# Up-projection weights loaded with a cast instead of converted beforehand, and late adaLN blocks moved behind an earlier sample tile

## The chip, the cores and the metric

The kernel runs on eight cores of one Trainium2 chip, the same program on each. A core has one prompt sequence (2048 tokens) and 16 sample sequences of 8 tokens (128 tokens). No data passes between the cores. The time is the device time in microseconds of the slowest core, as a median over runs; less is better. TensorE multiplies matrices, VectorE, ScalarE and GpSimd work on tiles, SyncE (SP) only issues transfers.

## The reference, cut to what matters

One layer with width 1024. Modulation vectors come from a conditioning vector (adaLN, six parts of 1024). Then a mixer with two halves, a gated linear recurrence and a short convolution, and an MLP with squared ReLU:

```python
mod = silu(c) @ w_ada + b_ada                       # sh1, sc1, g1, sh2, sc2, g2
h = rms_norm(x) * (1 + sc1) + sh1
q, fz, i, g, gb, gc, hv = split(h @ w_in)           # 7 blocks of 512 columns
logf = log(lb + (1 - lb) * sigmoid(fz)); k = 1 - exp(logf)
o, s_new = recurrence(q, k, logf, i, s0)            # 4 heads, state 128 x 128, chunks of 64 (8 for samples)
o_rec = rms_per_head(o) * g_onorm * silu(g)
o_conv = gb * short_conv(gc * hv)                   # width 3
x = x + g1 * (concat[o_rec, o_conv] @ w_out)
h2 = rms_norm(x) * (1 + sc2) + sh2
x = x + g2 * (square(relu(h2 @ w_up)) @ w_down)
y = rms_norm(x) * g_final
```

Prompt states start at zero; each sample sequence has its own start state (16 x 256 KB a core, read and written back).

## The kernel before, in words

**Stages.** First four blocks of `w_ada` are loaded and turned into shift and scale of the mixer. Then nine mixer tiles follow: eight prompt tiles of 256 tokens (p0 to p7) and one sample tile (s) of 128 tokens, in the order of the list `tiles` (line 1091). p0 and p1 run interleaved, the others follow each other, with `norm1` of the next tile put in front of each. A tile's projections come in the order F (forget gate, weight block 1), V (2), Q (0), G (3), then the recurrence R, then C (5), H (6), B (4), then the output projection. Its result goes to a DRAM scratch (`x1`). Last come six groups of up to three blocks of 128 tokens: `norm2`, `up` (8 weight blocks, in the order 1, 2, 0, 3, 5, 6, 4, 7), `down` (8 blocks).

**Weights in SBUF.** Every block of 128 x 4096 lies in DRAM as fp32 (2 MB) and in SBUF as bf16 (1 MB). A transfer that casts is issued by GpSimd. `wup` 0 to 6 takes the place of `win` 0 to 6, `wup7` that of `wout0`, so an up block can be loaded when the last prompt tile has read the projection block beneath it. `wdn` 0 and 1 lie where two `w_ada` buffers (`adaR`, line 563) and the ring of sample states (`SlR`, line 566) also lie; `wdn` 3 to 7 lie where tile buffers of the mixer were.

**Loads of the kernel before.** `convert(i)` (line 631) casts block i of `w_up` from DRAM to a bf16 scratch in DRAM (`wscr`), issued by GpSimd; `load_up` (line 636) copies it into SBUF on SP's queue, 1 MB. All eight up blocks go this way. `load_dn` (line 639) casts straight into SBUF, on GpSimd. The list `CONV` (line 1093) says how many conversions are written behind each tile; the first of a tile waits for the 21st TensorE operation of that tile, the others are given an empty slice of the list (it has fewer than 100 entries) and wait for no TensorE operation. Blocks 6 to 11 of `w_ada` (shift, scale and gate of the MLP) are loaded two at a time while p2 and p3 run: `late_mod` and `gates(1)`.

**What sets the order.** Every operation is written down with its reads, writes and a cost; `schedule` (line 125) then runs an event model and fixes the order of each engine's queue, first ready and then first written first. Each engine works through its queue in that order and waits in front of an operation whose inputs are not there. The model has transfers share the DMA engines: a transfer takes its bytes at 330 GB/s, GpSimd's queue gets 80% while SP or ScalarE has one too (lines 45 to 47, 147 to 151). An operation that reads what a transfer brings is planned 4 us after it. GpSimd's transfer number k waits for number k-6 (`SWDGE_DEPTH`, line 107). Dependences go by buffer names, so all of `modT` is one buffer: who reads any of it waits for every earlier write.

The profile names lines of helpers: L404 and L415 are matmuls and transposes, L431 ScalarE, L438, L442, L444, L448 and L452 VectorE or GpSimd, L465 transfers.

Of the kernel before, what the change touches and what calls it, by code (L numbers as in the profile page):

```python
# [368 lines left out]
def build_program():  # L369
    nc = bass.Bass("TRN2", target_bir_lowering=False)  # L370

    def din(name, shape):
        return nc.dram_tensor(name, shape, F32, kind="ExternalInput").ap()
# [8 lines left out]
    wup_d = din("w_up", [8, 128, 4096]); wdn_d = din("w_down", [8, 128, 4096])  # L382
# [3 lines left out]
    wscr_d = nc.dram_tensor("wscr", [16, 128, 4096], BF16, kind="Internal").ap()  # L386
# [3 lines left out]
    P = Prog(nc)  # L390
# [7 lines left out]
    def mm(specs, r, w, prio=None):  # L398
        specs = list(specs)

        def fn(e):
            ins = None
            for (o_, l_, r_, st, sp_) in specs:
                ins = e.matmul(o_, lhsT=l_, rhs=r_, start=st, stop=sp_, skip_group_check=True)  # L404
            return ins
        c = sum(max(nfree(s[2]) * 0.4167 + 2.5, 25.0) for s in specs)
        return P.op("pe", fn, r, w, c, prio=prio)
# [29 lines left out]
    def tt(eng, out, in0, in1, op, r, w, prio=None, mode=1.0):  # L437
        return P.op(eng, lambda e: e.tensor_tensor(out=out, in0=in0, in1=in1, op=op), r, w, vec_cost(eng, out, mode), prio=prio)  # L438

    def ts(eng, out, in0, s1, s2, op0, op1, r, w, prio=None, mode=2.0):  # L440
        if op1 is None:
            f = lambda e: e.tensor_scalar(out=out, in0=in0, scalar1=s1, scalar2=None, op0=op0)  # L442
        else:
            f = lambda e: e.tensor_scalar(out=out, in0=in0, scalar1=s1, scalar2=s2, op0=op0, op1=op1)  # L444
        return P.op(eng, f, r, w, vec_cost(eng, out, mode), prio=prio)
# [17 lines left out]
    def dma(eng, out, in_, r, w, nbytes, prio=None, after=()):  # L463
        c = {"pool": 1000.0, "sp": 600.0, "act": 100.0}[eng]
        o = P.op(eng, lambda e: e.dma_start(out=out, in_=in_), r, w, c, dma=float(nbytes), prio=prio)  # L465
        o.preds += [(d, True) for d in after]
        return o

    UPORD = (1, 2, 0, 3, 5, 6, 4, 7)
# [51 lines left out]
    wup, wup_n = [], []  # L521
# [46 lines left out]
    wdn, wdn_n = [], []  # L568
# [47 lines left out]
    MB2 = 1024 * 512 * 4  # L616
    ada_slot = {}
    flat = lambda t: t[:].rearrange("p k n -> p (k n)")

    def load_ada(j):  # L620
        t, n = (ada0R if j < 4 else adaR).take()
        ada_slot[j] = (t, n)
        dma("pool", flat(t), wada_d[j], [], [n], MB2)

    def load_in(j):
        dma("pool", flat(win[j]), win_d[j], [], [win_n[j]], MB2)
# [4 lines left out]
    def convert(i, after):  # L631
        dma("pool", wscr_d[i], wup_d[i] if i < 8 else wdn_d[i - 8], [], ["wscr%d" % i], 1.5 * MB2, after=after)

    up_ops = {}

    def load_up(j):
        up_ops[j] = dma("sp", flat(wup[j]), wscr_d[j], ["wscr%d" % j], [wup_n[j]], MB2 / 2)

    def load_dn(j):
        gate = up_ops.get(4 if j == 2 else 7)  # L640
        dma("pool", flat(wdn[j]), wdn_d[j], [], [wdn_n[j]], MB2, after=[gate] if gate else ())


    dma("pool", cB[:, 0:256], cB_d[:, 0:256], [], ["cB"], 128 * 1024)
# [29 lines left out]
    def mod_block(bi, first, j0, out_j0):  # L674
        if first:
            mod_bank[0] = UR.take()
        bank, bn = mod_bank[0]
        t, n = ada_slot[bi]
        c0 = 0 if first else 68
        for cj in range(4):  # L680
            col = c0 + cj * 17
            mm([(bank[:, col:col + 17], t[:, k, cj * 128:(cj + 1) * 128], scT[:, k, :], k == 0, k == 7) for k in range(8)],
               [n, "scT"], [bn])
        if not first:
            tt("dve", modT[:, out_j0:out_j0 + 8, :], bank[:, 0:136].rearrange("p (a b) -> p a b", b=17),
               badaT[:, j0:j0 + 8].unsqueeze(2).to_broadcast([128, 8, 17]), ALU.add, [bn, "vecT"], ["modT"])
            if out_j0 in (8, 24):
                ts("dve", modT[:, out_j0:out_j0 + 8, :], modT[:, out_j0:out_j0 + 8, :], 1.0, None, ALU.add, None, ["modT"], ["modT"])

    def gate_half(bi, g, half, gt, gt_n):  # L690
        t, n = ada_slot[bi]
        bank, bn = UR.take()
        mm([(bank[0:17, :], scT[:, k, :], t[:, k, :], k == 0, k == 7) for k in range(8)], [n, "scT"], [bn])
        c0 = half * 512
        tt("dve", gt[0:17, c0:c0 + 512], bank[0:17, :], gt[0:17, c0:c0 + 512], ALU.add, [bn, gt_n], [gt_n])

    def gates(g):
        gt, gt_n = xrR.take()
        src = bg_d[g * 1024:(g + 1) * 1024]
        dma("sp", gt[0:17, :], src.partition_broadcast(17), [], [gt_n], 17 * 4096)  # L700
        for half in range(2):
            gate_half((4 if g == 0 else 10) + half, g, half, gt, gt_n)
        dma("sp", gate_d[:, g * 1024:(g + 1) * 1024], gt[0:17, :], [gt_n], ["gated%d" % g], 17 * 4096)
# [37 lines left out]
    def norm1(kind, ti):  # L741
        hi = (0, 2, 1)[hcnt[0]] if hcnt[0] < 3 else (hcnt[0] + 1) % 2
        h, hn = hT[hi], "hT%d" % hi
        hcnt[0] += 1
        if kind == "s":
            nbv, nbn = normed(xs_d[:, :], [])
            sample_mod(nbv, nbn, h, hn, 0, 0, 8)
            return h, hn
        nbs = [normed(xp_d[(ti * 2 + b) * 128:(ti * 2 + b + 1) * 128, :], []) for b in range(2)]
        for jh in range(2):  # L750
            M, Mn = NR.take()
            Mb = M[:, :].bitcast(BF16)
            for b in range(2):
                tr([(Mb[:, j * 256 + b * 128:j * 256 + (b + 1) * 128], nbs[b][0][:, (jh * 4 + j) * 128:(jh * 4 + j + 1) * 128], ident)
                    for j in range(4)], [nbs[b][1], "cB"], [Mn])
            for j in range(4):
                jj = jh * 4 + j
                ts("dve", h[:, jj, :], Mb[:, j * 256:(j + 1) * 256], modT[:, 8 + jj, 0:1], modT[:, jj, 0:1], ALU.mult, ALU.add,
                   [Mn, "modT"], [hn], mode=1.0)
        return h, hn  # L760
# [327 lines left out]
    mod_block(3, False, 8, 8)  # L1088
    for j in (1, 2, 0, 3, 5, 6, 4):
        load_in(j)  # L1090
    tiles = [("p", 0), ("p", 1), ("p", 2), ("p", 3), ("s", 0), ("p", 4), ("p", 5), ("p", 6), ("p", 7)]
    hs = {}
    CONV = {5: 2, 6: 2, 7: 3, 8: 1}
    hs[0] = norm1(*tiles[0]); hs[1] = norm1(*tiles[1])
    load_ada(4); load_ada(5)
    load_out(0)
# [3 lines left out]
    conv_i = 0  # L1100

    def gen(n_):
        kind, ti = tiles[n_]
        return mixer_tile(kind, ti, kind == "p" and ti == 7, hs[n_][0], hs[n_][1], SAMPLE if kind == "s" else ti * 2)
# [9 lines left out]
    for g_ in (g0, g1):  # L1114
        for _ in g_:
            pass
    load_ada(6); load_ada(7)

    def late_mod(q):
        for i in range(2):  # L1120
            mod_block(6 + 2 * q + i, i == 0, 24 + 8 * q, 16 + 8 * q)

    for n_ in range(2, len(tiles)):
        t0op = len(P.ops)
        if n_ + 1 < len(tiles):
            hs[n_ + 1] = norm1(*tiles[n_ + 1])
        for step in gen(n_):
            if n_ == 2 and step == "Q":
                late_mod(0)
                load_ada(8); load_ada(9)  # L1130
            if n_ == 2 and step == "B":
                late_mod(1)
                load_ada(10); load_ada(11)
            if n_ == 3 and step == "Q":
                gates(1)
            if step == "B" and n_ + 1 == len(tiles):
                WB = View(wall[2:6])
                for j in UPORD[:7]:
                    load_up(j)
                norm2(bgroups[0])  # L1140
        pe_ops = [o for o in P.ops[t0op:] if o.eng == "pe"]
        for i in range(CONV.get(n_, 0)):
            convert(UPORD[conv_i], pe_ops[20 + 80 * i:21 + 80 * i])
            conv_i += 1
        if n_ == 6:
            load_dn(0); load_dn(1)
    load_up(7)
    load_gates(1)
    dma("sp", gfin_b[:], gfin_d.partition_broadcast(128), [], ["gfin_b"], 128 * 4096)
    for j in range(2, 8):  # L1150
        load_dn(j)
# [65 lines left out]
```

How the kernel before makes its waits and increments, by code:

```python
            def run(e, h):  # L325
                for o in order[e]:
                    for key, (val, d) in need_of[o.idx].items():
                        if d.chan is not None:
                            h.wait_ge(csem[key], val * 16)
                        else:
                            h.wait_ge(esem[key], d.cnt)
                    ins = o.fn(h)
                    if o.chan is not None:
                        ins.then_inc(csem[o.chan], 16)
                    elif o.signal:
                        ins.then_inc(esem[e], 1)
                if e == "sp":
                    for c, n in self.chans.items():
                        h.wait_ge(csem[c], n * 16)
```

## Time and profile before

| | |
|---|---|
| median of 3 runs | 929.48 us (927.96 to 930.94) |
| profiled execution | 927.96 us |
| its span, slowest core (5) | 926.4 us |
| spans of the cores | 914.6 to 926.4 us |
| TensorE busy | 826.0 us (89%) |
| VectorE, ScalarE, GpSimd busy | 466.9, 366.2, 166.8 us |
| DMA | 113.93 MB in packets, HBM read 129.56 MB |

Busy TensorE is a union of pipelined matmuls. The profile cuts the span in 40 slices of 23 us; TensorE is at nine tenths or more in most of them from the fourth on, and falls to 6 tenths with a granted clock of 6 tenths of full speed in the slice that begins near 417 us. The DMA engines are at 7 to 9 tenths in the first ten slices, at 3 and 4 in the next two, at 6 to 9 up to some 510 us, and at 0 to 2 from there.

### The profile page before, as it was taken

How to read it: one execution, taken by the hardware profiler on the slowest of the kernel's cores; microseconds unless marked ns; L12 is line 12 of the kernel's file. 1: busy time of each engine (PE TensorE's matmuls, PEld its weight loads, DVE VectorE, ACT ScalarE, POOL GpSimd, SP SyncE). 2: the span in 40 equal slices, each digit the busy share in tenths (PEclk: the TensorE clock that was granted, in tenths of full speed). 3: DMA queues.
4: the chain of work that ended last, by engine and by line, in shares of the span. 5: the costliest groups of instructions: out<-in, count | busy, mean ns of one | idle time of the engine just before them, and what ended most of it. 6: DMA issues, size and time to landing. Idle time of an engine off the chain costs nothing.

```text
span 926.4 us, 16715 instructions; the slowest of 8 cores (914.6 to 926.4 us)
## 1 busy us (share of the span) xinstructions
PE 826.0 (89%) x5929; PEld 513.6 (55%) x5929; DVE 466.9 (50%) x851; ACT 366.2 (40%) x780; POOL 166.8 (18%) x218
## 2 busy tenths in 40 slices
PE   0147999999898999986999999999999999999995
PEld 0124876777676657653654565456446545644862
DVE  0023597667879687685443445234514533442421
ACT  2036558374747567632330333133214312311411
POOL 2000022332153342242201200200120021002001
PEclk9997999999999999996999999999999999999998
DMA  8999789999346668798996211210221012002001
GB/s 161 215 183 196 137 161 162 201 181 235 112 149 239 140 174 201 188 241 187 227 195 157 95 43 47 91 69 2 91 69 46 24 46 91 2 1 83 31 2 45
DMA packets 27436, 113.93 MB, mean 123 GB/s; under 512 B 3845, under 2 KB 4229, under 8 KB 22362
## 3 DMA queue, kind: packets, MB, share of 16 engines
q0 software_dynamic: 4848, 39.19, 26.8%
q1 hardware_dynamic: 17610, 55.85, 18.9%
q10 hardware_dynamic: 4896, 17.83, 6.2%
q8 instruction: 48, 0.79, 0.3%
q14 instruction: 34, 0.28, 0.1%
HBM read 129.56 MB, written 30.88 MB: 173 GB/s over the span
## 4 chain that ended last, share of the span: by engine, by line
PE 75%; DVE 6%; DMA 6%; issue 6%; ACT 5%; ACTq 0%; POOL 0%; DVEq 0%; POOLq 0%
PE G L404 41%; PE U L404 23%; PE O L404 9%; DMA win_44<-w_in 5%; PE M L415 1%; DMA cB<-constB 1%; ACT W_140 L431 1%; DVE Sd_85 L438 1%; DVE h2T L444 1%; PE M L404 1%; DVE Ts_84 L438 1%; ACT Sb_86 L431 1%; ACT W_142 L431 0%; ACT W_141 L431 0%; ACT W_139 L431 0%
## 5 line engine op out<-in xcount | busy, mean ns | idle before, releaser
L444 DVE TENSOR_SCALAR h2T<-M,modT 128x128 bf16<-128x128 bf16 x128 | 43.9, 343 | 23.7 <-PE M L415 13.7
L431 ACT ACTIVATE W_140<-G 128x384 f32<-128x384 f32 (+2 forms) x38 | 19.7, 519 | 52.3 <-PE G L404 52.3
L415 PE MATMUL M<-cB,W_135 128*128 128x128 bf16 (+1 forms) x144 | 13.3, 231 | 30.1 <-DVE lnoml L438 20.9
L431 ACT ACTIVATE W_135<-xn_145 128x1024 bf16<-128x1024 f32 x17 | 17.9, 1053 | 45.6 <-PE M L415 36.2
L431 ACT ACTIVATE W_136<-xn_146 128x1024 bf16<-128x1024 f32 x17 | 17.9, 1053 | 25.7 <-PE M L415 15.8
L438 POOL TENSOR_TENSOR xr_147<-xr_147,W_138 128x512 f32<-128x512 f32 x8 | 10.5, 1312 | 97.1 <-DVE W_138 L438 96.9
L415 PEld LDWEIGHTS M<-cB,W_135 128*128 128x128 bf16 (+1 forms) x144 | 9.9, 104 | 32.6 <-issue 31.2
L431 ACT ACTIVATE Sb_86<-Sd_85 128x512 bf16<-128x512 f32 x16 | 10.0, 627 | 37.8 <-DVE Sd_85 L438 37.8
L438 POOL TENSOR_TENSOR xr_147<-xr_147,W_137 128x512 f32<-128x512 f32 x5 | 6.3, 1267 | 102.6 <-DVE W_137 L438 102.6
L438 DVE TENSOR_TENSOR uT<-W_138,G 128x384 bf16<-128x384 f32 (+1 forms) x26 | 13.7, 528 | 17.2 <-ACT W_138 L431 16.6
L404 PE MATMUL G<-hT_60,win_44 128*128 128x256 bf16 x128 | 18.4, 303 | 4.4 <-DMA win_44<-w_in 4.4
L431 ACT ACTIVATE W_137<-G 128x384 f32<-128x384 f32 (+1 forms) x24 | 11.4, 475 | 25.8 <-PE G L404 25.0
L438 DVE TENSOR_TENSOR Ts_84<-Sd_85,U 128x512 f32<-128x512 f32 x31 | 21.1, 682 | 0.7
L431 ACT ACTIVATE W_140<-W_140 128x512 f32<-128x512 f32 x32 | 20.1, 630 | 2.1
L404 PE MATMUL G<-wdn_129,uT 128*128 128x512 bf16 x88 | 20.8, 379 | 0.0
L404 PE MATMUL G<-wdn_128,uT 128*128 128x512 bf16 x88 | 20.8, 379 | 0.0
L404 PE MATMUL G<-wdn_127,uT 128*128 128x512 bf16 x88 | 20.8, 379 | 0.0
L404 PE MATMUL G<-wdn_130,uT 128*128 128x512 bf16 x88 | 20.8, 379 | 0.0
L438 DVE TENSOR_TENSOR uT<-W_137,G 128x384 bf16<-128x384 f32 (+1 forms) x24 | 12.9, 537 | 15.6 <-ACT W_137 L431 14.1
L431 ACT ACTIVATE W_138<-G 128x384 f32<-128x384 f32 (+1 forms) x26 | 12.2, 469 | 21.0 <-PE G L404 21.0
L438 DVE TENSOR_TENSOR uT<-W_139,G 128x384 bf16<-128x384 f32 (+1 forms) x24 | 13.0, 542 | 14.5 <-ACT W_139 L431 14.5
L438 DVE TENSOR_TENSOR W_138<-U,Gp 128x512 f32<-128x512 f32 x16 | 11.0, 687 | 16.3 <-PE U L404 15.0
(565 smaller groups left out, 2149.0 us busy)
## 6 DMA issues: line engine op xcount, KB each, us to landing
wscr<-w_up POOLq DMA_DIRECT2D x8, 1024.0 KB, 14.9
xn_146<-x ACTq DMA_DIRECT2D x9, 512.0 KB, 4.7
xn_145<-xp ACTq DMA_DIRECT2D x8, 512.0 KB, 11.0
xn_146<-xp ACTq DMA_DIRECT2D x8, 512.0 KB, 9.6
ada_111<-w_ada POOLq DMA_DIRECT2D x4, 1024.0 KB, 13.4
ada_112<-w_ada POOLq DMA_DIRECT2D x4, 1024.0 KB, 22.5
xn_145<-x ACTq DMA_DIRECT2D x8, 512.0 KB, 3.4
xr_148<-xp SPq DMA_DIRECT2D x6, 512.0 KB, 14.7
```

The costliest lines, as they stand in the source:

```text
L404: ins = e.matmul(o_, lhsT=l_, rhs=r_, start=st, stop=sp_, skip_group_check=True)
L415: ins = e.transpose(out=o_, in_=i_, identity=id_)
L431: return P.op("act", lambda e: e.activation(out=out, in_=in_, func=func, **kw), r, w, c, prio=prio)
L438: return P.op(eng, lambda e: e.tensor_tensor(out=out, in0=in0, in1=in1, op=op), r, w, vec_cost(eng, out, mode), prio=prio)
L444: f = lambda e: e.tensor_scalar(out=out, in0=in0, scalar1=s1, scalar2=s2, op0=op0, op1=op1)
```

## The change

The order of the engines is planned by the same `schedule` with the same costs. What is written down changes:

- up blocks: `load_up` casts straight from fp32 into SBUF on GpSimd's queue (2 MB read); no conversion of `w_up` is left.
- down blocks 4 to 7 are converted in DRAM beforehand (`CONV` is now a list of scratch blocks 12 to 15), one behind each of the tiles number 5 to 8 of the list (counted from 0), each waiting for the 21st TensorE operation of its tile; `load_dn` copies them on SP's queue, each chained to the SP transfer written before it. Down blocks 0 to 3 stay casting loads on GpSimd; 0 and 1 are written behind tile number 7.
- the sample tile comes fourth instead of fifth.
- blocks 6 to 11 of `w_ada` are loaded behind the tiles number 4, 5 and 6; their matmuls come behind tiles 5 and 6, `gates(1)` behind tile 7. As `adaR` shares SBUF with `SlR`, they can be loaded only when the sample tile is through with its states.

```diff
     def load_up(j):
-        up_ops[j] = dma("sp", flat(wup[j]), wscr_d[j], ["wscr%d" % j], [wup_n[j]], MB2 / 2)
+        dma("pool", flat(wup[j]), wup_d[j], [], [wup_n[j]], MB2)

     def load_dn(j):
-        gate = up_ops.get(4 if j == 2 else 7)
-        dma("pool", flat(wdn[j]), wdn_d[j], [], [wdn_n[j]], MB2, after=[gate] if gate else ())
+        if 8 + j in CONV:
+            dma("sp", flat(wdn[j]), wscr_d[8 + j], ["wscr%d" % (8 + j)], [wdn_n[j]], MB2 / 2, after=[o for o in P.ops if o.dma and o.eng == "sp"][-1:])
+        else:
+            dma("pool", flat(wdn[j]), wdn_d[j], [], [wdn_n[j]], MB2)
...
-    tiles = [("p", 0), ("p", 1), ("p", 2), ("p", 3), ("s", 0), ("p", 4), ("p", 5), ("p", 6), ("p", 7)]
+    tiles = [("p", 0), ("p", 1), ("p", 2), ("s", 0), ("p", 3), ("p", 4), ("p", 5), ("p", 6), ("p", 7)]
-    CONV = {5: 2, 6: 2, 7: 3, 8: 1}
+    CONV = [12, 13, 14, 15]
...
-    load_ada(6); load_ada(7)
-
-    def late_mod(q):
-        for i in range(2):
-            mod_block(6 + 2 * q + i, i == 0, 24 + 8 * q, 16 + 8 * q)
-
     for n_ in range(2, len(tiles)):
...
         for step in gen(n_):
-            if n_ == 2 and step == "Q":
-                late_mod(0)
-                load_ada(8); load_ada(9)
-            if n_ == 2 and step == "B":
-                late_mod(1)
-                load_ada(10); load_ada(11)
-            if n_ == 3 and step == "Q":
-                gates(1)
...
-        pe_ops = [o for o in P.ops[t0op:] if o.eng == "pe"]
-        for i in range(CONV.get(n_, 0)):
-            convert(UPORD[conv_i], pe_ops[20 + 80 * i:21 + 80 * i])
+        mark = [o for o in P.ops[t0op:] if o.eng == "pe"][20:21]
+        if n_ in (5, 6):
+            for i in range(2):
+                mod_block(4 + 2 * (n_ - 4) + i, i == 0, 24 + 8 * (n_ - 5), 16 + 8 * (n_ - 5))
+        if n_ == 7:
+            gates(1)
+            load_dn(0); load_dn(1)
+        if n_ in (4, 5, 6):
+            load_ada(6 + 2 * (n_ - 4)); load_ada(7 + 2 * (n_ - 4))
+        if 5 <= n_ and conv_i < 4:
+            convert(CONV[conv_i], mark)
             conv_i += 1
-        if n_ == 6:
-            load_dn(0); load_dn(1)
```

## Rows read from the trace of the kernel before

**Rows 1.** Spans of the cores: span, mean granted TensorE clock.

```profile
core 5: 926.4 us, clock 0.979
```

**Rows 2.** Busy us by stretch: length, PE, PEld, DVE, ACT, POOL, clock, DMA share, GB/s.

```profile
120.00:240.00 120.00, 116.65 (x1189) 86.10 (x1188) 88.91 (x157) 69.78 (x142) 33.98 (x55) 1.00 0.93 188
240.00:320.00 80.00, 70.61 (x660) 52.27 (x657) 64.02 (x115) 52.35 (x107) 34.02 (x44) 0.98 0.50 153
320.00:400.00 80.00, 75.89 (x651) 54.01 (x649) 61.47 (x99) 53.80 (x105) 25.50 (x38) 1.00 0.78 196
400.00:437.00 37.00, 25.48 (x163) 13.79 (x162) 27.01 (x49) 11.02 (x24) 12.82 (x12) 0.77 1.00 192
437.00:520.00 83.00, 82.22 (x463) 44.09 (x462) 31.06 (x65) 20.03 (x44) 9.94 (x11) 1.00 0.77 171
```

**Rows 3.** Waits of TensorE, 400 to 437 us: us in total, times, longest.

```profile
PE U L404 <- POOL mix_152 L438: 2.8, 1, 2.8
```

**Rows 4.** DMA queues: packets, MB, share of 16 engines over the span.

```profile
q0 software_dynamic: 4848, 39.19, 26.8%
q1 hardware_dynamic: 17610, 55.85, 18.9%
```

**Rows 5.** DMA issues, 437 to 520 us: KB each, us from issue to landing.

```profile
wdn_129<-w_down POOLq DMA_DIRECT2D x1, 1024.0 KB, 15.8
...
wdn_134<-w_down POOLq DMA_DIRECT2D x1, 1024.0 KB, 48.5
...
gfin_b<-g_final SPq DMA_DIRECT2D x1, 512.0 KB, 27.1
```

**Rows 6.** GpSimd in order of time: start us, us, what.

```profile
443.23 0.60 POOL L465 DMA_DIRECT2D wdn_129<-w_down  x1 [7.23 <-DMA recp<-rout]
...
450.99 0.57 POOL L465 DMA_DIRECT2D wdn_134<-w_down  x1
```

**Rows 7.** TensorE in order of time, tiles p6 and p7 and first MLP group.

```profile
323.82 1.91 PE L404 MATMUL G<-hT_60,win_44 128*128 128x256 bf16 x16
...
364.34 1.04 PE L404 MATMUL G<-hT_61,win_44 128*128 128x256 bf16 x8
...
375.03 1.91 PE L404 MATMUL G<-hT_61,win_44 128*128 128x256 bf16 x16
...
379.47 1.89 PE L404 MATMUL G<-win_45,hT_61 128*128 128x512 bf16 x8
...
398.22 1.89 PE L404 MATMUL U<-wout_50,mix_83 128*128 128x512 bf16 x8
...
410.21 1.04 PE L404 MATMUL G<-hT_61,win_47 128*128 128x256 bf16 x8
...
437.02 4.06 PE L404 MATMUL G<-h2T,wup_53 128*128 128x384 bf16 x24
...
473.42 1.46 PE L404 MATMUL U<-h2T,wup_59 128*128 128x384 bf16 x8
...
517.16 1.89 PE L404 MATMUL O<-wdn_134,uT 128*128 128x512 bf16 x8
```

**Rows 8.** Waits of GpSimd, whole span: us in total, times, longest.

```profile
POOL win_48 L465 <- DMA adaf_109<-w_ada: 10.6, 1, 10.6
```

**Rows 9.** GpSimd in order of time, two places.

```profile
316.35 0.59 POOL L465 DMA_DIRECT2D wdn_127<-w_down  x1 [5.02 <-DMA recs<-Sl_119]
...
396.81 0.72 POOL L438 TENSOR_TENSOR mix_83<-W_137,sg_80 128x256 bf16<-128x256 f32 x1
```

**Rows 10.** TensorE in order of time: a late adaLN block and half a gate.

```profile
170.18 0.96 PE L404 MATMUL U<-scT,ada_111 128*128 128x17 bf16 x32
...
211.49 1.90 PE L404 MATMUL U<-ada_111,scT 128*17 128x512 bf16 x8
```

**Rows 11.** DMA issues, 110 to 250 us: KB each, median us to landing.

```profile
ada_112<-w_ada POOLq DMA_DIRECT2D x3, 1024.0 KB, 21.0
```

**Rows 12.** Waits of TensorE, whole span.

```profile
PE U L404 <- DMA adaf_109<-w_ada: 10.1, 1, 10.1
```

More of the change, by code:

```diff
@@ L632, in convert @@
         dma("pool", wscr_d[i], wup_d[i] if i < 8 else wdn_d[i - 8], [], ["wscr%d" % i], 1.5 * MB2, after=after)
-    up_ops = {}
     def load_up(j):
-        up_ops[j] = dma("sp", flat(wup[j]), wscr_d[j], ["wscr%d" % j], [wup_n[j]], MB2 / 2)
+        dma("pool", flat(wup[j]), wup_d[j], [], [wup_n[j]], MB2)
     def load_dn(j):
-        gate = up_ops.get(4 if j == 2 else 7)
-        dma("pool", flat(wdn[j]), wdn_d[j], [], [wdn_n[j]], MB2, after=[gate] if gate else ())
+        if 8 + j in CONV:
+            dma("sp", flat(wdn[j]), wscr_d[8 + j], ["wscr%d" % (8 + j)], [wdn_n[j]], MB2 / 2, after=[o for o in P.ops if o.dma and o.eng == "sp"][-1:])
+        else:
+            dma("pool", flat(wdn[j]), wdn_d[j], [], [wdn_n[j]], MB2)
     dma("pool", cB[:, 0:256], cB_d[:, 0:256], [], ["cB"], 128 * 1024)
```

## The prediction

> **What bounds the kernel now.** I read the spans of the cores first: core 5 is the slowest, 926.4 us at a mean granted clock of 0.979 [rows 1]. The profiled execution took 927.96 us, so 1.6 us lie outside the span, and the median of the three runs, 929.48 us, is 1.5 us above it. The sum below is made against 927.96 and then moved up by those 1.5 us.
>
> The busy time by stretch is the second view, and the reader should see three stages in it [rows 2]. From 520 us on (the MLP groups) the matmul engine hardly idles; the same weights lie in SBUF in both kernels, so nothing of this change reaches that part. From 120 to 400 us (mixer tiles) it is nearly full: idle 3.35 of 120 us, then 9.4 of 80 around the sample tile, then 4.1 of 80. From 400 to 437 us, the end of the last prompt tile, 11.5 of 37 us are idle and the granted clock is 0.77, a mix of 2.4 and 1.2 GHz after the engine had begun to wait. So all that can be won before the MLP is about 28 us of idle time and a few us at the lower clock. The waits of that last stretch are the third view: the longest is 2.8 us for GpSimd's product into `mix` [rows 3], the rest are links of the same chain on VectorE and ScalarE, and no weight load stands in the list.
>
> The queues are the fourth view [rows 4]. 26.8% of 926.4 us for 37 casting transfers on GpSimd's queue (39.19 MB written) is 248 / 37.4 = 6.6 us of all sixteen engines for each. The plain queue of SP takes 18.9% for 55.85 MB, 3.1 us a MB, so 3.3 us for a 1.05 MB block that is already bf16.
>
> **The change, part by part.**
>
> *Up weights.* Eight plain copies of 3.3 us on SP become eight casting loads of 6.6 us on GpSimd; 26 us more engine time, in the stretch where the DMA share is 1.00 already [rows 2]. What pays for it: eight conversions in DRAM go, four (of `w_down`) come, and four `w_down` loads become plain copies. Do the loads come late? In the kernel before, six casting loads that follow each other land between 443.23 + 15.8 = 459.0 and 450.99 + 48.5 = 499.5 us, 8.1 us apart [rows 5, 6]. The first weight block is free when its last reader in tile p7 ends, 376.9 us, the second at 381.4, the seventh at 411.3 [rows 7]. At 15.8 us for the first and 8.1 for each further one they land at 393, 401, 409, 417, 425, 433 and 441, and with one conversion between (449) the eighth, free at about 437, lands at 457. They are needed from 437.0, one each (473.42 - 437.02) / 7 = 5.2 us, the eighth at 473.4 [rows 7]. The tightest has 16 us left: cost 0. The work that hides them is the rest of tile p7. The two `w_down` blocks behind them land by 465 and 473, and are needed from about 517.2 - 5 x 5.2 = 491 [rows 7]. The four plain copies are chained behind the copy of the final gain, which took 27.1 us from its issue near 440 [rows 5]: 467, then even 10 us each gives 507 for the last, needed at 517 [rows 7].
>
> *GpSimd's order.* GpSimd issues in order, and its DMA number k waits until number k-6 has landed. Such a wait is seen at the start: 10.6 us in front of `win_48` for a load six issues back [rows 8]. There nothing stood behind it. In tile p7 eleven issues now stand between GpSimd's products into `mix` and its residual adds, for which the output projection waits. Most find their sixth predecessor long landed. One does not: the last conversion comes six behind the second up load. The order is planned with 2 MB at 330 GB/s and 80% of the engines, 7.9 us a load with 3.1 us of overhead in all, so this load lands at about 377 + 2 x 7.9 + 3 = 395 in the plan; by the rows it is 401. The plan can thus put the conversion in front of the product that ends at 397.5 and that the output projection at 398.2 waits for [rows 7, 9]. A wait of some 5 us there stops TensorE for 5 us, as the kernel before shows in small at 316.35, where a `w_down` issue held an add back for 5.0 us [rows 9]. Bounds: 0 if the conversion is planned elsewhere, 10.6 by the wait at the start. I take +5.
>
> *Late adaLN blocks.* Blocks 6 to 11 are loaded behind the sample tile now, since their two buffers share SBUF with the sample states. A prompt tile less ahead of it, 364.34 - 323.82 = 40 us [rows 7], and the landing of the sample tile's last store, at 316 us in the kernel before [rows 9], comes near 276. Then follow load, matmuls, load, matmuls, load, gates: three rounds. TensorE's own work is the same, 4 x 0.82 us and 2 x 1.9 us [rows 10], about 7 us. A round's second load takes 21.0 us to land [rows 11]; the plan allows about the same. `norm1` of p6 and p7 also waits for these blocks, as one buffer name covers all of `modT`; 276 + 21 = 297 and some 320 lie ahead of 323.8 and 364.3, where their projections begin, so this is covered. What is left is TensorE standing in front of a block that is late. Bounds: 0, and 10.1, the longest wait for such a block at the start [rows 12]. I take +2, nearer to the stretch 120 to 240 us, where six of these loads passed without such a wait.
>
> *Relief in the early tiles.* Three ungated conversions and six adaLN loads leave 120 to 240 us, where the DMA share is 0.93 [rows 2]. The engine idles 3.35 us there, mostly behind VectorE and ScalarE. Bounds -3.35 and 0; I take -1.
>
> *Moved work.* The 7 us of adaLN matmuls go from a stretch with 3% idle to one with 8% (13.5 of 160 us) and can lie in its gaps. The sample tile takes its 9.4 us of gaps along. Bounds -9.4 and +9.4, as these gaps can shrink or repeat; I take -2, a third of the moved work hidden.
>
> Sum: 0 + 5 + 2 - 1 - 2 = +4 us, 927.96 + 4 = 932.0 for such an execution, 933.5 us as a median.
>
> **A rule against the change.** The rows around 437 to 520 us give a casting load 8.1 us beside plain copies [rows 5, 6]. The Trainium skill, "DMA: Bandwidth & Descriptors", section "Queues, rings and completion order", says that each DMA engine takes turns between the rings that have work, packet by packet. By that rule GpSimd's queue would get half while SP's or ACT's has work, not the 80% of the plan. The pace that this would give is the first rival; the 8.1 us agree with it only where the plain queues are mostly empty.
>
> **The rivals.**
>
> *Weights late, slower.* If a casting load gets half of the engines during the whole of tile p7, it takes 13.2 us [rows 4]: 393, 406, 419, 432, 446, 459, then the conversion at 472, the seventh at 485, the eighth at 498. The sixth still makes it (needed at 463), the seventh is 17 us late and the eighth 25 us: 958 us, or 953 with part of it made up. It decides from about 10 us a load. For it: the DMA share of 1.00 in 400 to 437 [rows 2]. Against: the plain queues lose the eight copies in this very stretch, and have only residual blocks left.
>
> *Faster.* The plain queue, free of eight copies, and ScalarE's issues behind it no longer lengthen the chain of 400 to 437 us; 5 of its 11.5 idle us go, with 3 us of the early relief: 921.5 us. For it: idle time and the clock in that stretch [rows 2, 3]. Against: the longest wait there ends with GpSimd, whose queue gets more to do.
>
> *No change.* The loads were hidden and are hidden again, and the orders differ without effect: 929.5 us. For it: no wait for an up weight before, a margin of 16 us after. Against: the order of every engine is planned anew, and 28 us of gaps can move.
>
> **How the numbers follow.** The forecast gets 0.44, late weights 0.10, faster 0.28, no change 0.18. Within 0.3% (2.8 us) is what a measurement of this kernel cannot tell from no change; 0.06 of the forecast's chance lies there, so slower is 0.38 + 0.10 = 0.48, same 0.24, faster 0.28. The likeliest case's own range is 929 to 941. Its lower end must go on to the faster case with some of the gaps closed, 917, and its upper end to most of the late weights, 951.
>
> **What would show it.** Right: in the profile after, GpSimd waits several us in front of `wscr`, with `mix` products behind it and TensorE waiting for `mix` in tile p7; no wait of TensorE for `wup`; DMA share well under 0.9 in the early tiles and near 1 from 270 to 470 us; the first up matmul some 4 us later than 437. Wrong: a wait for `wup` or `wdn` (late weights), a first up matmul before 433 (faster), or a start of the MLP that moved for another reason, such as gaps at the sample tile.

## The result and the profile after

The changed kernel takes 958.69 us as a median (955.48 to 962.98, 4 runs), the kernel before 928.72 us beside it: 1.0326 times as long, interval 1.0274 to 1.0377. It is slower, as was likeliest, but by 30 us where 4 were forecast, and outside the range. In some executions the cores of one die run at a lower granted clock and the time is longer; all ratios here, and the medians given for e10 and e14, are over the other executions. The profiled execution, 962.98 us, is the longest of the four; its slowest core is core 2, against [rows 1].

```profile
core 2: 961.4 us, clock 0.960
```

The busy time by stretch has the columns of [rows 2] (length, PE, PEld, DVE, ACT, POOL, clock, DMA share, GB/s), so that each row can be held against its counterpart.

```profile
120.00:240.00 120.00, 107.56 (x1067) 81.42 (x1076) 101.58 (x174) 76.23 (x154) 48.64 (x64) 0.96 0.51 153
240.00:320.00 80.00, 76.23 (x701) 55.74 (x707) 56.80 (x98) 47.54 (x96) 27.17 (x37) 1.00 0.50 124
320.00:400.00 80.00, 73.76 (x673) 54.54 (x677) 52.92 (x91) 47.42 (x100) 27.47 (x37) 0.99 0.88 168
400.00:437.00 37.00, 28.74 (x201) 19.08 (x202) 26.07 (x51) 11.17 (x23) 6.79 (x11) 0.78 1.02 178
437.00:520.00 83.00, 50.24 (x281) 27.96 (x280) 23.32 (x47) 19.09 (x42) 7.12 (x8) 0.79 0.89 199
```

The last row is the place. TensorE idles 32.8 of 83 us there, 0.8 before. From 120 to 437 us little is lost in sum: 120 to 240 us lose 9.1 (the sample tile lies there now), 240 to 320 win 5.6, 320 to 400 lose 2.1, 400 to 437 win 3.3. TensorE in order of time around 437 us (start, us, what, idle time before and its releaser) shows how it stops.

```profile
434.26 4.06 PE L404 MATMUL G<-h2T,wup_53 128*128 128x384 bf16 x24
...
448.12 2.72 PE L404 MATMUL U<-h2T,wup_54 128*128 128x384 bf16 x8 [8.50 <-DVE W_137 L438]
...
454.74 1.46 PE L404 MATMUL U<-h2T,wup_52 128*128 128x384 bf16 x8
...
480.76 2.72 PE L404 MATMUL G<-h2T,wup_52 128*128 128x384 bf16 x8 [22.82 <-DVE uT L438]
```

The up projection begins 2.8 us earlier than before [rows 7], stops twice, for 8.5 and 22.8 us, and behind each stop the same eight matmuls take 2.72 instead of 1.46 us (1.2 and 2.4 GHz). Both profiled cores are the latest of their eight. Over all cores the up projection begins at 420.5 to 434.3 us, before at 423.7 to 437.0 (medians 422.3 and 430.5), and from its first matmul to the first of `down` it takes 79 to 84 us, before 42 to 44. Every core has both stops, of 8.5 to 11.8 and 21.3 to 24.1 us. No up block is waited for. Who is? ScalarE, whose ReLU stands between a PSUM bank and VectorE's square, names GpSimd:

```profile
448.68 0.49 ACT L431 ACTIVATE W_138<-G 128x384 f32<-128x384 f32 x1 [25.13 <-POOL xr_148 L438]
...
479.47 0.49 ACT L431 ACTIVATE W_139<-G 128x384 f32<-128x384 f32 x1 [21.33 <-POOL xr_149 L438]
```

and GpSimd, in order of time, names a transfer:

```profile
408.14 0.51 POOL L465 DMA_DIRECT2D wscr<-w_down  x1 [13.45 <-PE O L404]
...
423.94 0.73 POOL L465 DMA_DIRECT2D wup_55<-w_up  x1
445.92 1.25 POOL L438 TENSOR_TENSOR xr_148<-xr_148,W_137 128x512 f32<-128x512 f32 x1 [21.25 <-DMA xr_148<-xp]
...
449.09 0.54 POOL L465 DMA_DIRECT2D wup_59<-w_up  x1
478.12 1.26 POOL L438 TENSOR_TENSOR xr_149<-xr_149,W_139 128x512 f32<-128x512 f32 x1 [28.49 <-DMA xr_149<-xp]
```

So the chain is: the residual rows of p7 (`xr<-xp`, a plain load on SP's queue) come late; GpSimd's residual adds wait; the product tiles W_137 to W_139 that the adds read are also tiles of the up projection's ReLU (`WB` and `WT` are views of one array), so ScalarE, VectorE and at last TensorE stop. SP in order of time says when the loads were issued:

```profile
356.03 0.26 SPq L465 DMA_DIRECT2D xr_147<-b_gate  x1
389.18 0.33 SPq L465 DMA_DIRECT2D x<-xr_148  x1
...
400.56 0.24 SPq L465 DMA_DIRECT2D gates<-xr_147  x1
407.06 0.33 SPq L465 DMA_DIRECT2D xr_148<-xp  x1
410.82 0.61 SPq L465 DMA_DIRECT2D convp<-uco  x1
414.05 0.34 SPq L465 DMA_DIRECT2D xr_149<-xp  x1
```

The late MLP gate holds xr_147, one of three residual buffers, from 356 to 400 us, so p7's loads wait until p6's stores (389 and 392) have landed. The gate's matmuls run only at 390 to 393.6, and its bias, 17 rows of 4 KB issued at 356.0, is in use on VectorE only at 399.0; VectorE waits 8.1 us for it, and TensorE 3.3 behind that. From 370 to 393 us SP's queue moved next to nothing (packets, MB, share):

```profile
q1 hardware_dynamic: 14, 0.05, 1.4%
```

That is a packet every 1.6 us, as if the rows came one after the other. Then p7's loads are slow too: the second is issued at 414.05 and releases GpSimd at 478.1, 64 us later, behind the store of the convolution's last rows (`convp`, 4 KB in 512 pieces of 8 bytes). The queues in 424 to 446 us (packets, MB, share of 16 engines) and some issues of 395 to 440 us (KB, us to landing) tell more.

```profile
q0 software_dynamic: 283, 2.52, 75.3%
q10 hardware_dynamic: 272, 1.02, 17.2%
q1 hardware_dynamic: 286, 0.06, 2.3%
```

```profile
wup_55<-w_up POOLq DMA_DIRECT2D x1, 1024.0 KB, 38.1
xr_148<-xp SPq DMA_DIRECT2D x1, 512.0 KB, 38.7
...
Gs<-gates SPq DMA_DIRECT2D x1, 512.0 KB, 48.4
...
recp<-rout SPq DMA_DIRECT2D x1, 256.0 KB, 50.1
...
convp<-uco SPq DMA_DIRECT2D x1, 4.0 KB, 61.9
```

GpSimd's casting queue, ScalarE's and SP's moved nearly the same number of packets. But a casting packet held an engine 0.753 x 16 x 22 / 283 = 0.94 us on average, one of ScalarE's 0.22, one of SP's 0.03. If the three take turns, a turn is 1.2 us, and in it SP's queue moves one packet, of 8 bytes if that is what lies in front. By this estimate 512 pieces on 16 engines are 32 turns, 38 us, for 4 KB.

The first residual load lies ahead of these pieces in SP's queue and took 38.7 us all the same. The 0.06 MB in SP's row are some 14 rows of 4 KB beside pieces of 8 bytes. Ahead of that load lies the gate's store (400.56), 17 rows again; if these also go one after the other, part of the load comes behind them. This is read from the trace and tested by no run.

In the kernel before `recp<-rout` took 21.9 us beside one conversion (issues of 405 to 437 us), and p7's last residual load was in use at 443.9, 6.5 us after its issue (SP in order of time): no casting load was in flight then.

```profile
recp<-rout SPq DMA_DIRECT2D x1, 256.0 KB, 21.9
```

```profile
437.36 0.33 SPq L465 DMA_DIRECT2D xr_149<-xp  x1
```

### The profile page after: what moved, and what is told of

Read it like the earlier page. It is cut to its first block, busy times and chain, and to the rows that moved or that the text cites. A ratio compares the mean times of both kernels' runs of the same rounds, so it can differ in the third digit from the quotient of the medians.

```text
span 961.4 us, 16637 instructions; the slowest of 8 cores (948.8 to 961.4 us)
## 1 busy us (share of the span) xinstructions
PE 823.5 (86%) x5873; PEld 517.7 (54%) x5929; DVE 465.1 (48%) x851; ACT 363.9 (38%) x780; POOL 171.7 (18%) x218
## 3 DMA queue, kind: packets, MB, share of 16 engines
q0 software_dynamic: 5232, 39.19, 25.1%
## 4 chain that ended last, share of the span: by engine, by line
PE 67%; DMA 13%; DVE 6%; issue 5%; ACT 4%; another core or an unknown queue 3%; POOL 2%; POOLq 0%; ACTq 0%; DVEq 0%; SPq 0%
PE G L404 37%; PE U L404 20%; PE O L404 8%; DMA win_44<-w_in 5%; DMA xr_148<-xp 4%; DMA x<-xr_148 2%; PE M L415 1%; DMA cB<-constB 1%; DVE h2T L444 1%; ACT W_140 L431 1%; DMA Sl_120<-srec 1%; DVE Sd_85 L438 1%; DMA recs<-Sl_118 1%; DMA recs<-Sl_120 0%
## 5 line engine op out<-in xcount | busy, mean ns | idle before, releaser
L444 DVE TENSOR_SCALAR h2T<-M,modT 128x128 bf16<-128x128 bf16 x128 | 43.9, 343 | 22.9 <-PE M L415 13.0
L404 PE MATMUL G<-h2T,wup_52 128*128 128x384 bf16 (+1 forms) x96 | 16.6, 329 | 22.8 <-DVE uT L438 22.8
L431 ACT ACTIVATE W_138<-G 128x384 f32<-128x384 f32 (+1 forms) x26 | 12.2, 469 | 40.7 <-POOL xr_148 L438 25.1
L431 ACT ACTIVATE W_139<-G 128x384 f32<-128x384 f32 (+1 forms) x24 | 11.6, 482 | 38.7 <-POOL xr_149 L438 21.3
L404 PEld LDWEIGHTS G<-h2T,wup_52 128*128 128x128 bf16 x96 | 9.6, 101 | 28.4 <-issue 24.0
L438 DVE TENSOR_TENSOR W_137<-U,Gp 128x512 f32<-128x512 f32 x13 | 9.0, 689 | 28.0 <-PE U L404 14.2
L431 ACT ACTIVATE W_137<-G 128x384 f32<-128x384 f32 (+1 forms) x24 | 11.4, 476 | 27.4 <-PE G L404 24.4
L438 DVE TENSOR_TENSOR uT<-W_138,G 128x384 bf16<-128x384 f32 (+1 forms) x26 | 13.7, 528 | 15.3 <-ACT W_138 L431 14.7
L404 PE MATMUL G<-wdn_128,uT 128*128 128x512 bf16 x87 | 20.7, 379 | 0.1
L404 PE MATMUL G<-wdn_130,uT 128*128 128x512 bf16 x87 | 20.7, 379 | 0.1
L404 PE MATMUL G<-wdn_129,uT 128*128 128x512 bf16 x86 | 20.7, 379 | 0.1
```

The lines of the kernel that those rows point to most:

```text
L431: return P.op("act", lambda e: e.activation(out=out, in_=in_, func=func, **kw), r, w, c, prio=prio)
```

## The experiments

Ratios are to the kernel before, run on the same chip; medians of different runs can come from different chips. The first two take a link out of this chain.

**The 512-piece store out of the way (e1).** Order of PE, VectorE and GpSimd unchanged.

```diff
-        if last or kind == "s":
-            dma("sp", convp_d[...] if kind == "p" else convs_d[...], ...)
+        if kind == "s": dma("sp", convs_d[:, :, :], uco[:], ...)
...
-            dma("sp", xr[:], src, [], [xrn], 128 * 4096)
+            xload = dma("sp", xr[:], src, [], [xrn], 128 * 4096)
+            if last and b == NB - 1: dma("sp", convp_d[:, :, :], uco[:, :, 0:2], ..., after=[xload])
```

> The changed kernel, with the 4 KB store of the last convolution rows held until the last residual load of tile p7 has landed; the order of TensorE, VectorE and GpSimd is the same. Theory: in tile p7 the casting loads hold the DMA engines, a plain queue gets one packet per engine and turn (286 packets on 16 engines from 424 to 446 us, 1.2 us each), and the store's 512 packets of 8 bytes stand ahead of the last residual load (issued 414, landed about 478 us). Without them that load lands by 445, TensorE's wait of 22.8 us goes, up blocks that land at 462 and 470 cost 5 to 8 us of it again: 942 to 946 us. Rival one, the plain queue is starved by bytes, not by packets: the load still takes 60 us, 957 to 960 us. Rival two, the up weights are late whatever the residual does: the wait moves from the squares to the up blocks, 952 to 960 us.

938.7 us, 1.0143 (1.0122 to 1.0163): 20 us of the 30 go when 4 KB move aside, more than expected. The second residual load now takes 38 us from issue (409.1) to use, not 64, less of a gain than the 38 us estimated for the pieces; GpSimd waits 3.9 us for it instead of 28.5. The wait for the first load stays (23.1 us, TensorE 10.4 behind it). And TensorE now meets up blocks that come late, once for 3.4 us and once for 0.7:

```profile
PE G L404 <- DMA wup<-w_up: 3.4, 1, 3.4
```

**Own product tiles for p7 (e2).** The adds still wait, but hold nothing of the up projection.

```diff
+    WL = View(wall[10:13])
-                W, Wn = WT.take()
+                W, Wn = (WL if last else WT).take()
```

> The changed kernel, with the residual products of tile p7 in three tiles of their own instead of three of the four that the up projection also turns over. Theory: TensorE stood for 8.5 and 22.8 us because two, then four of these tiles waited for GpSimd's adds, and these for starved residual loads. With tiles of their own the adds are as late as before (446 and 478 us) and TensorE doesn't wait for them; it meets the up blocks instead, the fourth landing at 462 (needed at 450) and the fifth near 470: 12 to 15 us stay, 941 to 947 us. Rival, the tiles are not the link: the waits stay, 957 to 960 us. If the weights were no limit at all: 927 to 932 us.

940.16 us, 1.0159 (1.0139 to 1.0179), just under what was expected, and not with the waits that were expected: no up block is waited for. GpSimd still waits 55.4 us for residual rows; TensorE now waits 13.2 us for the last of its own product tiles and 5.2 for a down block issued behind the adds. So both links are real: late plain transfers, and shared tiles that pass the wait on.

**The weight part alone (e3) and the order alone (e4).** e3 is the kernel before with `load_up`, `load_dn` and `CONV` of the change; e4 the changed kernel with these three as before.

```diff
-    CONV = {5: 2, 6: 2, 7: 3, 8: 1}     # e3; e4 the other way round
+    CONV = [12, 13, 14, 15]
```

> The kernel before with the weight part alone: up blocks cast straight into SBUF on GpSimd's queue, down blocks 4 to 7 through the scratch; tile order and adaLN loads as before. Theory: this part makes the loss, 948 to 960 us, with residual loads of p7 that take 30 us and more and GpSimd waiting for them. Rival, the sample tile in fourth place and the late adaLN blocks make it: 927 to 934 us.

> The changed kernel with the weights of the kernel before (eight up blocks through the scratch and SP's queue, all down blocks cast by GpSimd); the sample tile fourth and adaLN blocks 6 to 11 late, as in the change. Theory: 927 to 936 us (gaps at the sample tile 9 us more from 120 to 240 us and 6 less from 240 to 320). Rival, this part makes the loss: 945 to 960 us.

The theory fell twice. e3 takes 913.76 us, 0.9883 (0.9855 to 0.9912): the weight part by itself is a gain. e4 takes 964.87 us, 1.0429 (1.0403 to 1.0455): the order loses more without them. e3 by stretch (columns as above), then GpSimd in order of time:

```profile
400.00:437.00 37.00, 28.43 (x183) 16.35 (x182) 24.65 (x49) 12.15 (x26) 10.25 (x11) 0.86 1.01 170
437.00:520.00 83.00, 82.22 (x459) 43.69 (x458) 34.74 (x67) 23.41 (x55) 9.56 (x8) 1.00 0.72 183
```

```profile
424.12 1.28 POOL L438 TENSOR_TENSOR xr<-xr,W 128x512 f32<-128x512 f32 x1
449.30 1.10 POOL L465 DMA_DIRECT2D wdn<-w_down  x2 [23.89 <-DMA recp<-rout]
```

GpSimd waits 23.9 us for a plain store here too, but its last residual add is done at 425.4, and only down blocks stand behind. TensorE, which begins the up projection at 422.66 us, does not notice. In e4 TensorE waits for the gate's sum with its bias (waits of 395 to 520 us: total, times, longest), and SP in order of time shows that bias issued behind three weight copies, and the gate's store and the residual load later still:

```profile
PE U L404 <- DVE xr L438: 28.1, 2, 27.9
```

```profile
378.64 8.58 SPq L465 DMA_DIRECT2D wup<-wscr  x3
387.32 3.00 SPq L465 DMA_DIRECT2D xr<-b_gate  x1
...
442.38 5.74 SPq L465 DMA_DIRECT2D gates<-xr  x1
461.33 0.34 SPq L465 DMA_DIRECT2D xr<-xp  x1
```

**The two halves of the order.** e5: weight part and sample tile fourth, adaLN blocks early as before. e6: weight part and late adaLN blocks, sample tile fifth.

```diff
-    tiles = [("p", 0), ("p", 1), ("p", 2), ("s", 0), ("p", 3), ...]     # e6
+    tiles = [("p", 0), ("p", 1), ("p", 2), ("p", 3), ("s", 0), ...]
```

> The kernel before with the weight part and the sample tile fourth; the adaLN blocks 6 to 11 stay early, around p2. The weight part alone took 913.8 us, the rest of the change alone 964.9. Theory: the loss is the late adaLN blocks (the last gate holds a residual buffer in tile p6 to p7, and the first two down blocks wait for it and fall among the up blocks); the sample tile moves only gaps: 910 to 922 us. Rival, the earlier sample tile makes the loss: 940 to 960 us.

> The changed kernel with the sample tile back in fifth place; its adaLN blocks 6 to 11 come behind that tile, so up to one prompt tile later still. Theory: late adaLN blocks make the loss, and later ones cost as much or more: 955 to 985 us. Rival, the earlier sample tile makes the loss: 912 to 930 us.

e5: 942.7 us, 1.0128 (1.0098 to 1.0157), a miss. e6: 956.08 us, 1.0271 (1.0242 to 1.03), as expected. In e5 the residual loads are in time; its longest waits of GpSimd for a transfer and of TensorE (total, times, longest) are

```profile
POOL wdn L465 <- DMA recp<-rout: 26.9, 1, 26.9
```

```profile
PE G L404 <- DVE uT L438: 23.7, 1, 23.7
```

It is e3's wait for the final state's store, but here the last residual add was planned behind it. In e6 GpSimd waits 24.1 and 29.7 us for residual rows, and TensorE 24.9 and 12.2.

**The gate off the residual buffers (e7), the two down blocks behind the up blocks (e8).**

```diff
-        gt, gt_n = xrR.take()                                            # e7
+        gt, gt_n = xrR.take() if g == 0 else (gfin_b, "gfin_b")
...
-            load_dn(0); load_dn(1)                                       # e8
-    for j in range(2, 8):
+    for j in range(8):
```

> The changed kernel with the second gate built in the buffer of the final gain instead of one of the three residual buffers. Theory: this takes one of the two late residual loads of tile p7 (issued at 407 and 414 us behind a gate that was stored at 400 us) forward by a tile, GpSimd's first wait of 21 us goes and the second ends when the first did, near 446 us: 934 to 944 us. Rival, the loads are late only for want of DMA turns: 950 to 960 us.

> The changed kernel with down blocks 0 and 1 written behind the eight up blocks instead of behind tile p6, so that they don't stand among the up loads; GpSimd issues as many casting loads as before. Theory: up blocks come up to 16 us earlier but the casting queue is full until about 477 us all the same, the residual loads land as late and GpSimd's adds hold the tiles: 952 to 962 us. Rival, the up blocks set the time: 938 to 946 us.

e7: 938.39 us, 1.0084 (1.005 to 1.0118): 20 of the 30 us go with the buffer. GpSimd no longer waits for residual rows but 15.4 us for the gate's store to DRAM, another plain transfer, and TensorE 19.8 us for what stands behind, then 5.0 us for an up block. e8: 961.57 us, 1.0328 (1.0283 to 1.0373): as long as the residual rows hold GpSimd (54.3 us here), the place of the down blocks does not matter.

**The store in 128 pieces of 32 bytes (e9).** The last rows are gathered in a contiguous tile. Every engine's order stays; only the size of the pieces changes.

```diff
-                if last:
-                    copy("pool", uco[:, ccs[0]:ccs[0] + 2, 0:2], uv[:, :, 256:258], [ubn], ["uco"])
-                else:
-                    copy("pool", uc[...], uv[:, :, 256:258], [ubn], [ucn])
+                copy("pool", uc[...], uv[:, :, 256:258], [ubn], [ucn])
...
+        if last:
+            dma("sp", convp_d.rearrange("p c t -> p (c t)"), uc[:].rearrange("p c t -> p (c t)"), ...)
```

> The changed kernel, in which the store of the last two convolution rows reads a contiguous tile: 128 pieces of 32 bytes instead of 512 pieces of 8, same bytes, same place in every queue; the order of all engines is the same. Theory (a plain queue gets one packet per engine and turn while casting loads run, 1.2 us each): 384 / 16 = 24 turns or 29 us fewer ahead of the last residual load, so it lands near 449 instead of 478 us, and the time is that of the run with the store held back, 936 to 943 us. Rival, the place of the store counted, not its pieces: 954 to 960 us.

939.3 us, 1.0123 (1.0081 to 1.0165), as expected: same bytes, a quarter of the pieces, 19 us. GpSimd's waits, 380 to 560 us, and the store's own row:

```profile
POOL xr L438 <- DMA xr<-xp: 33.6, 2, 23.6
```

```profile
convp<-uc SPq DMA_DIRECT2D x1, 4.0 KB, 43.9
```

33.6 us of waiting are left of 49.8: the wait for the second load fell from 28.5 to 10.0 us, the one for the first stayed (23.6).

**The packed store in the other corners (e10, e11, e14).** The same edit on e5, on e3 and on e6.

> Weights and sample tile fourth (942.7 us), with the same store in 128 pieces. There GpSimd waited 26.9 us in front of a down block for the store of the final state, which is queued behind that store, and TensorE 23.7 us for the adds behind it. Theory: with 24 turns fewer that wait falls under 5 us and the loss goes: 915 to 923 us. Rival, the early sample tile costs by itself: 938 to 944 us.

> The weight part alone (913.8 us), with the same store in 128 pieces. There GpSimd waited 23.9 us for the store of the final state as well, but the residual adds stood ahead of that wait, and TensorE didn't wait. Theory: no gain beyond 3 us, 909 to 914 us. Rival, the store's pieces slow every kernel alike: 885 to 895 us.

> Weight part and late adaLN blocks, sample tile still fifth, with the packed store; without packing this kernel took 956.1 us. Theory (late adaLN blocks cost what they cost through the plain queue of SP, which is behind in the last prompt tile): 15 to 20 us less, 936 to 942 us. Rival (their cost lies elsewhere, in matmuls and weight loads that come late): 950 us or more.

| with the weight part | 512 pieces | 128 pieces |
|---|---|---|
| sample fifth, adaLN early | 0.9883 (0.9855 to 0.9912) | 0.9839 (0.9818 to 0.9861) |
| sample fourth, adaLN early | 1.0128 (1.0098 to 1.0157) | 0.9973 (0.9955 to 0.9991) |
| sample fifth, adaLN late | 1.0271 (1.0242 to 1.03) | 1.0196 (1.0153 to 1.0238) |
| both (the change) | 1.0326 (1.0274 to 1.0377) | 1.0123 (1.0081 to 1.0165) |

Packing gains where GpSimd's residual adds stand behind a plain transfer. Where they don't (e11 against e3), no gain is shown: 913.89 and 913.76 us, and the intervals of the ratios overlap. The weight part alone, with or without packing, is the fastest of these kernels. e10, 926.99 us, came down by 16 us, not the 20 to 27 forecast. e14 is the miss that counts: 949.64 us, 6 us less than e6 (0.75% by the ratios), where 15 to 20 were expected, and at the 950 of its rival, by which the cost of late adaLN blocks lies elsewhere. Its waits for residual rows went from 53.8 to 33.5 us, but GpSimd's wait for `recp` grew to 22.6 and TensorE waited 7.3 us for an up block issued behind the first of the adds:

```profile
PE U L404 <- DMA wup<-w_up: 7.3, 1, 7.3
```

**Two half-cures at once.** e12 is e9 with e7's edit, e13 is e9 with e2's.

> The changed kernel with the store in 128 pieces and the second gate in the buffer of the final gain, so that no residual buffer waits for it. Theory: both links of the late residual loads are gone; what is left is gaps at the sample tile (some 4 us) and the down blocks 0 and 1 among the up blocks: 914 to 928 us. Rival, the up blocks themselves are late after that: 932 to 940 us.

> Both earlier half-cures at once: the packed last conv-row store, and own tiles for the residual products of the last prompt tile. The packed kernel alone took 939.3 us and still showed TensorE waiting 10.9 us for a product tile of VectorE and 5.6 us for the squares. Theory (those waits exist only because GpSimd's adds hold the tiles of the up projection): they go, 922 to 932 us. Rival (each cure uncovers the next plain transfer or weight load, which is nearly as late): 934 to 941 us, with a new wait of TensorE in 430 to 500 us.

e12: 940.88 us, 1.0134 (1.0108 to 1.016). e13: 941.17 us, 1.009 (1.0062 to 1.0118). Neither adds up; both lie at the upper edge of what their rivals gave (932 to 940, 934 to 941), and TensorE waits 6.3 and 5.7 us for up blocks in them. In e12 the longest waits of GpSimd and TensorE that took the place are

```profile
POOL mix L438 <- DMA gates<-gfin_b: 15.2, 1, 15.2
```

```profile
PE M L415 <- DVE W L438: 18.4, 1, 18.4
```

**Casting loads held back (e15).** The five last up blocks wait until p7's second residual load has landed. The 512 pieces stay.

```diff
-                for j in UPORD[:7]:
+                for j in UPORD[:3]:
...
-    load_up(7)
+    for j in UPORD[3:]:
+        load_up(j, after=xloads[-1:])
```

> The changed kernel with the casting loads of up blocks 4 to 8 held until the last residual load has landed; the conv-row store stays in 512 pieces of 8 bytes in front of it in SP's queue. Theory (the plain queue is slow only because casting loads have the DMA engines): that load lands in 25 to 40 us instead of 64, GpSimd waits under 8 us for it, and TensorE waits 15 to 25 us in all for up blocks instead; 945 to 960 us, near the changed kernel. Rival (the plain queue is slow by itself, from the small pieces): the load still takes 55 us or more, the held blocks come later still, 970 us or more.

956.3 us, 1.0254 (1.0227 to 1.0281). That load is issued at 407.7 us and releases GpSimd at 445.4, after a wait of 0.9 us: 37.7 us instead of 64, as the theory said.

```profile
445.38 2.70 POOL L465 DMA_DIRECT2D wup<-w_up  x5 [0.90 <-DMA xr<-xp]
```

The clearest rows are of transfers issued on SP at 433 to 438 us, when the last casting load before the hold was about done (KB, us to landing):

```profile
Gs<-gates SPq DMA_DIRECT2D x1, 512.0 KB, 13.1
...
recp<-rout SPq DMA_DIRECT2D x1, 256.0 KB, 11.3
```

48.4 and 50.1 us in the changed kernel: the plain queue is slow beside casting loads, not by itself. The wait for the first residual load, 26.0 us, stayed; casting loads issued up to 415 us were still under way, and the gate's rows lie ahead of it here too. TensorE paid 14.7 us for up blocks that now came late.

## Why the prediction was wrong, point by point

*Up weights, cost 0.* The pace was right, the cost by luck. `wup_53` landed at 372.8 + 25.1 = 397.9 us, `wup_59` at 449.1 + 27.6 = 476.7 with nine loads between: 7.9 us each where 8.1 were taken. But the step counted one conversion between the up blocks, and two down blocks came among them as well. The fourth block in use, `wup_55`, landed at 423.9 + 38.1 = 462.0; at 5.2 us a block from 434.3 it was needed near 450. TensorE waited for none because it stood for the product tiles at that time. Where these stops shrink, it waits for up blocks: 4.1 us in e1, 5.0 in e7, 6.3 in e12, 5.7 in e13, 7.3 in e14, 14.7 in e15. By itself the weight part gains 1.2% (e3), which was nearest to the rival *faster*: in e3 the up projection begins at 418.8 to 422.7 us on the eight cores (median 421.6, before 430.5) and lasts as long as before, and 400 to 437 us, where that rival saw its gain, show 3 us more work at a higher clock. What the step left out besides is what these loads do to others.

*GpSimd's order, +5.* Wrong in kind. The conversion did wait, 13.45 us, but for TensorE, on whose 21st operation of the tile it is made to wait, not for a landing. TensorE stood 3.0 us for a product into `mix`, before 2.8 [rows 3], and the up projection began earlier. The example at 316.35 [rows 9] was misread: an add was held for 5.0 us there, but TensorE went on. GpSimd did become the bound, but from 424.7 us on and through another transfer. That the kernel is slower, as forecast, is luck: the 5 us that made the forecast did not occur, and the first up matmul came before 433 us on seven of eight cores, the prediction's own sign of *faster*.

*Late adaLN blocks, +2 with bounds 0 and 10.1.* This is the step that failed. It costs 1.0271 - 0.9883 = 0.039, some 36 us, with the weight part (e6 against e3). The prediction looked only for TensorE standing in front of such a block, at the price of [rows 12]. No row of after has such a wait from 240 to 520 us. The step did not follow two other ways: the gate's buffer is one of three residual buffers (without that, e7, 20 of the 30 us go), and the loads that this delays go through SP's queue while casting loads hold the engines (e1 and e9, 20 and 19 us). The two do not add up (e12), and with the packed store the late blocks still cost 1.0196 - 0.9839 = 0.036, 33 us (e14 against e11): the pieces of the store are not the price of these blocks. In the rival *weights late* it even said that the plain queues "have only residual blocks left", as if those were harmless.

*Moved work, -2.* Failed as well. The gaps of the sample tile did move as the bounds had it (+9.1 and -5.6 us in the trace). But moving the tile costs 0.0245, 23 us, with the weight part (e5 against e3): the plan put GpSimd's last residual adds behind a wait for `recp`. With the packed store 0.0134 is left (e10 against e11), and a wait of 12.0 us. With the late blocks in, the move costs only 0.0055: the costs do not add, as when both end in the same waits of GpSimd for SP's queue.

*Early relief, -1.* Not seen by itself; the sample tile fills that stretch now.

*The rivals.* *Weights late* gave 953 to 958 us, near the time measured, but its wait for up blocks does not occur in the changed kernel. It occurs, with 4 to 15 us, in versions whose stops are shorter. *Faster* holds for the weight part alone.

*The rule.* The Trainium skill, "DMA: Bandwidth & Descriptors", section "Queues, rings and completion order", says that an engine takes turns between rings, packet by packet. The 283, 272 and 286 packets agree. What the prediction drew from it, half of the engines for GpSimd, does not follow: the turns were equal in number, not in time, and a casting packet took 0.94 us of the 1.2 us turn. The rule spoke against this change, but on SP's side.

*What stays open.* With the late blocks no version came below 1.0084. In e14 TensorE idles 13.1 us in 400 to 437 us and 20.4 in 437 to 520, against 8.3 and 1.0 in e11; each cure let the next plain transfer (gate, residual rows, final state) or a block issued behind it come last. A version in which GpSimd waits for no plain transfer at all in 400 to 480 us was not run, so that this is the whole of the 36 us is argued, not shown. Two rivals for the rest stand untested: up blocks that are late by themselves, since e8, which takes the two down blocks out of their way, was run only where the residual rows still held GpSimd; and the gate's transfers of 17 rows, which no run splits differently.

## What to carry to other kernels

When a change puts casting loads into a stretch, list the plain transfers of the same stretch and who waits for them in an in-order queue, and price them by turns: pieces divided by engines, times the length of a turn beside a casting packet. This is a rough estimate: it gave 38 us here where 26 were gained without the pieces (e1). Follow a moved step through the buffers that it borrows and the plain transfers that it makes, not only through its inputs. A wait that does not occur may be covered by a longer one; see whether it appears when that one goes. Test the parts of a large change apart: here one part gains 1.2% and the others turn it into a loss of 3.3%.

## What the runs showed of the hardware that was not expected

A store of 4 KB in 512 pieces took 61.9 us, in 128 pieces 43.9, and the whole kernel 19 us less. Beside casting loads 512 KB on a plain queue took 38.7 to 64 us, with these held back 13.1. Three queues with work moved 283, 272 and 286 packets in 22 us while they held 75.3, 17.2 and 2.3% of the engines' time. A load of 17 rows of 4 KB took 43 us to its use beside casting loads, with SP's queue moving 14 packets in 23 us.
